# The first job of a transformer block on one core: 512 columns first, x from a second queue, and the operand split straight from PSUM

## The reference

```
xn   = rms_norm(x, norm_mix_g)
proj = xn @ w_in        # split: q_a k_a v_a | q_b k_b v_b | g_a g_b
o_a  = mixer_a(...)     # 16 heads of 64 on 2 key heads, window of 2 chunks, sink, t5 bias
o_b  = mixer_b(...)     # 16 heads of 64, chunks to the left, relative bias
merged = sigmoid(g_a) * (o_a @ w_branch_a) + sigmoid(g_b) * (o_b @ w_branch_b)
h    = x + merged @ w_out
hn   = rms_norm(h, norm_ffn_g)
out  = h + (silu(hn @ w_ffn_gate) * (hn @ w_ffn_up)) @ w_ffn_down
```

## Time and profile before

| | us |
|---|---|
| median of 3 runs (1349.22 to 1349.34) | 1349.26 |
| span of the profiled execution | 1347.3 |
| PE busy | 1331.1 (99%) |
| DVE busy | 743.3 (55%) |
| ACT busy | 606.4 (45%) |
| POOL busy | 33.5 (2%) |
| DMA: 251.23 MB, mean | 186 GB/s |

### The profile page before, as it was taken

The page is one execution under the profiler, slowest core; times in us unless marked ns, Lnnn a source line. Parts: engine busy times, 40 slices in busy tenths (PEclk is TensorE's granted clock), DMA queues, the critical chain, the costliest instruction groups (busy, mean ns, idle before and its releaser), DMA issues.

```text
span 1347.3 us, 16021 instructions
## 1 busy us (share of the span) xinstructions
PE 1331.1 (99%) x6224; PEld 1100.3 (82%) x6224; DVE 743.3 (55%) x938; ACT 606.4 (45%) x781; POOL 33.5 (2%) x34
## 2 busy tenths in 40 slices
PE   7999999999999999999999999999999999999998
PEld 6888887777788888888888888888888888888887
DVE  6556556777455555565555555455545554555553
ACT  5454545555444444444444443344444434444442
POOL 1112110000000000000000000000000000000000
PEclk9999999999999999999999999999999999999999
DMA  8655655444565555555565555555555556555552
GB/s 260 198 202 165 210 188 182 147 148 143 206 200 188 188 187 188 188 185 187 188 193 185 191 188 201 194 188 188 189 186 188 187 200 196 195 187 187 187 187 94
DMA packets 129943, 251.23 MB, mean 186 GB/s; under 512 B 4624, under 2 KB 10832, under 8 KB 129632
## 3 DMA queue, kind: packets, MB, share of 16 engines
q1 hardware_dynamic: 129600, 250.37, 56.5%
q0 software_dynamic: 288, 0.10, 0.1%
HBM read 248.33 MB, written 2.12 MB: 186 GB/s over the span
## 4 chain that ended last, share of the span: by engine, by line
PE 95%; ACT 3%; DVE 1%; issue 0%; DMA 0%; DVEq 0%; SPq 0%; ACTq 0%
PE bank L948 30%; PE bank L950 30%; PE bank L949 30%; PE bank L877 2%; ACT prob L594 1%; PE bank L892 1%; ACT w_hi L494 1%; PE bank L917 1%; DVE staged L657 0%; PE bank L919 0%; PE bank L902 0%; DMA x_rows<-in_x 0%; PE bank L918 0%; DVE xT_lo L665 0%; DVE w_lo L648 0%
## 5 line engine op out<-in xcount | busy, mean ns | idle before, releaser
L648 DVE TENSOR_TENSOR w_lo<-raw,w_hi 128x1024 fp32r<-128x1024 f32 (+1 forms) x464 | 562.5, 1216 | 556.1 <-ACT w_hi L494 554.2
L494 ACT ACTIVATE w_hi<-raw 128x1024 fp32r<-128x1024 f32 (+1 forms) x464 | 487.6, 1052 | 694.8 <-PE bank L950 693.2
L948 PE MATMUL bank<-w_hi,xT_hi 128*128 128x512 f32 (+1 forms) x1248 | 488.6, 391 | 4.2 <-DVE w_lo L648 3.0
L950 PE MATMUL bank<-w_lo,xT_hi 128*128 128x512 f32 (+1 forms) x1248 | 483.2, 387 | 0.0
L949 PE MATMUL bank<-w_hi,xT_lo 128*128 128x512 f32 (+1 forms) x1248 | 482.9, 387 | 0.0
L948 PEld LDWEIGHTS bank<-w_hi,xT_hi 128*128 128x128 f32 x1248 | 234.9, 188 | 53.7 <-issue 2.6
L950 PEld LDWEIGHTS bank<-w_lo,xT_hi 128*128 128x128 f32 x1248 | 234.9, 188 | 47.9
L949 PEld LDWEIGHTS bank<-w_hi,xT_lo 128*128 128x128 f32 x1248 | 235.1, 188 | 45.8
L948 PE MATMUL bank<-w_hi,oT_hi 128*128 128x512 f32 x480 | 187.0, 390 | 0.0
L950 PE MATMUL bank<-w_lo,oT_hi 128*128 128x512 f32 x480 | 186.8, 389 | 0.0
L949 PE MATMUL bank<-w_hi,oT_lo 128*128 128x512 f32 x480 | 186.7, 389 | 0.0
(11 more groups left out here) (109 smaller groups left out, 496.2 us busy)
## 6 DMA issues: line engine op xcount, KB each, us to landing
raw<-in_w_in SPq DMA_DIRECT2D x64, 1024.0 KB, 5.3
raw<-in_w_ffn_gate SPq DMA_DIRECT2D x44, 1024.0 KB, 5.2
raw<-in_w_ffn_up SPq DMA_DIRECT2D x44, 1024.0 KB, 5.1
raw<-in_w_ffn_down SPq DMA_DIRECT2D x44, 1024.0 KB, 5.0
raw<-in_w_out SPq DMA_DIRECT2D x16, 1024.0 KB, 5.0
raw<-in_w_branch_a SPq DMA_DIRECT2D x8, 1024.0 KB, 5.0
raw<-in_w_branch_b SPq DMA_DIRECT2D x8, 1024.0 KB, 4.9
x_rows<-in_x SPq DMA_DIRECT2D x4, 512.0 KB, 7.7
```

The lines of the kernel that those rows point to most:

```text
L494: A(w_hi[:, p % SPLIT_SLOTS, 0:w], raw[:, c % RAW_SLOTS, (p % 2) * w:(p % 2 + 1) * w], ACT.Copy).then_inc(hi_ready, 1)
L648: V.tensor_tensor(w_lo[:, p % SPLIT_SLOTS, 0:w], raw[:, p // 2 % RAW_SLOTS, (p % 2) * w:(p % 2 + 1) * w], w_hi[:, p % SPLIT_SLOTS, 0:w].bi ...
L948: M(sums, x_hi, w_hi[:, p % SPLIT_SLOTS, w], start=kt == 0, stop=False)
L950: ins = M(sums, x_hi, w_lo[:, p % SPLIT_SLOTS, w], start=False, stop=kt == j.kts - 1)
```

## The change

Four edits.

- `plan` puts the first 512-column qk job ahead of the kv job. The other jobs stay as they are.
- x and the norm weights (`mix_rows`) are loaded from ACT's queue, all at the start of ACT's program, instead of from SP's between the weight chunks.
- PE transposes x and h two k-tiles to a bank, all tokens of each, instead of four k-tiles of one half of the tokens. ACT reads the bank with the norm weight as scale into the `_hi` tile (`gained_to_hi`), and DVE multiplies the bank by the weight and subtracts the `_hi` tile in one instruction (`gained_to_lo`). `staged` is out of this path. In the first job this comes after the split of an even piece instead of ahead of it.
- The norm-weight transpose moves ahead of the first quarter of x, the third and fourth quarters are transposed after pieces 1 and 3 instead of 0 and 2, and the squares of x are summed in the second job's first two pieces.

The diff, cut to its core:

```diff
-    job("kv", 0, "w_in", 0, qa, 2 * kva, kt, "x", 0)
     for n in range(qa // COLS):
         job("qk", n, "w_in", 0, n * COLS, COLS, kt, "x", 0)
+        if n == 0:
+            job("kv", 0, "w_in", 0, qa, 2 * kva, kt, "x", 0)
...
             def do_job(j):
                 for q in range(j.pieces // 2):
-                    if j.prev is None:
-                        cs = slice(q * COLS, (q + 1) * COLS)
-                        sp.dma_start(x_rows[:, :, cs], x_view[:, :, cs]).then_inc(x_landed[q], 16)
                     load_chunk(j, q)
...
+            def gained_to_hi(first_bank, kt0, g0, pair0):
+                for i in range(GROUP // 2):
+                    act.wait_ge(x_turned, pair0 + i + 1)
+                    for c in range(2):
+                        kt = 2 * i + c
+                        ins = A(xT_hi[:, kt0 + kt, :], bank[first_bank + i][:, c * S:(c + 1) * S], ACT.Copy,
+                                scale=g_col[:, g0 + kt:g0 + kt + 1])
+                    ins.then_inc(gained_hi, 1)
...
-                if j.kind == "out" and k == 6:
-                    scaled_to_hi(NB + j.n, j.n)
+                if j.kind == "out" and k == 5:
+                    gained_to_hi(T_BANK, j.n * GROUP, KT + j.n * GROUP, KT // 2 + 2 * j.n)
...
+            act.dma_start(mix_rows[:], norm_mix_g[0].rearrange("(k p) -> k p", p=P)).then_inc(mix_landed, 16)
+            for q in range(NB):
+                cs = slice(q * COLS, (q + 1) * COLS)
+                act.dma_start(x_rows[:, :, cs], x_view[:, :, cs]).then_inc(x_landed[q], 16)
...
                 for k in range(j.pieces):
+                    split_hi(j, k)
                     if j.prev is None and k % 2 == 0:
-                        scaled_to_hi(k // 2, k // 2)
-                    split_hi(j, k)
-                    if j.prev is None and k in (5, 7):
+                        gained_to_hi(4 + 2 * (g % 2), g * GROUP, g * GROUP, 2 * g)
+                    if j.prev is jobs[0] and k < T:
...
+            def gained_to_lo(first_bank, kt0, g0, pair0):
+                for i in range(GROUP // 2):
+                    dve.wait_ge(gained_hi, pair0 + i + 1)
+                    for c in range(2):
+                        kt = 2 * i + c
+                        ins = V.scalar_tensor_tensor(xT_lo[:, kt0 + kt, :], bank[first_bank + i][:, c * S:(c + 1) * S],
+                                                     g_col[:, g0 + kt:g0 + kt + 1],
+                                                     xT_hi[:, kt0 + kt, :].bitcast(F32), ALU.mult, ALU.subtract)
+                    ins.then_inc(xT_ready, 1)
...
                 p = j.piece0 + k
                 hi, lo = lhs[j.lhs]
                 pe.wait_ge(lo_ready, p + 1 + j.off)
+                if j.prev is None:
+                    pe.wait_ge(xT_ready, k + 1)
...
-            turn_x(0)
             pe.wait_ge(mix_landed, 16)
             turn(bank[0][:, 0:KT], mix_rows[:], ident[0:KT, 0:KT]).then_inc(g_turned, 1)
+            turn_x(0)
             turn_x(1)
...
-                    if j.prev is None and k in (0, 2):
-                        turn_x(k // 2 + 2)
+                    if j.prev is None and k in (1, 3):
+                        turn_x((k - 1) // 2 + 2)
```

More of the change, by code:

```diff
@@ L135, in plan @@
             j.set = sets
-            sets += 1
+            sets += j.kind != "out"
     at = 0
@@ L611, in do_job @@
                 for k in range(j.pieces):
+                    split_hi(j, k)
                     if j.prev is None and k % 2 == 0:
[L613 to L615 removed]
+                        if k == 0:
+                            act.wait_ge(g_ready, 1)
+                        g = k // 2
+                        gained_to_hi(4 + 2 * (g % 2), g * GROUP, g * GROUP, 2 * g)
+                    if j.prev is jobs[0] and k < T:
                         for q in range(NB):
                             act.wait_ge(x_landed[q], 16)
[L618 to L620 removed]
+                        A(squares[:, k, :], x_rows[:, k, :], ACT.Square,
+                          accum_out=x_ss[:, k:k + 1]).then_inc(x_ss_ready, 1)
                     if j.prev is not None:
@@ L650, in split_lo @@
                                 w_hi[:, p % SPLIT_SLOTS, 0:w].bitcast(F32), ALU.subtract).then_inc(lo_ready, 1)
[L652 to L667, removed]
-                                ALU.subtract).then_inc(xT_ready, 1)
+            def gained_to_lo(first_bank, kt0, g0, pair0):
[7 more added lines that the diff above has]
+                    ins.then_inc(xT_ready, 1)
             def turned_to_lo(dst_hi, dst_lo, at_group, sets_before, ready):
@@ L733, in follow @@
                     if k == 5:
-                        dve.wait_ge(turned, j.set + 1)
-                        scale_rows(T_BANK, KT + j.n * GROUP, NB + j.n)
+                        gained_to_lo(T_BANK, j.n * GROUP, KT + j.n * GROUP, KT // 2 + 2 * j.n)
                         if j.n == NB - 1:
@@ L862, in turn_x @@
                 pe.wait_ge(x_landed[g], 16)
-                if g >= 2:
-                    pe.wait_ge(scaled_ready, g - 1)
-                for t in range(T):
-                    for c in range(GROUP):
-                        ins = turn(bank[4 + 2 * (g % 2) + t][:, c * P:(c + 1) * P],
-                                   x_rows[:, t, g * COLS + c * P:g * COLS + (c + 1) * P], ident[:])
-                ins.then_inc(x_turned, 1)
+                for i in range(GROUP // 2):
+                    if g >= 2:
+                        pe.wait_ge(xT_ready, 2 * (g - 2) + i + 1)
+                    for c in range(2):
+                        for t in range(T):
+                            col = g * COLS + (2 * i + c) * P
+                            ins = turn(bank[4 + 2 * (g % 2) + i][:, c * S + t * P:c * S + (t + 1) * P],
+                                       x_rows[:, t, col:col + P], ident[:])
+                    ins.then_inc(x_turned, 1)
             def turn_set(j):
                 pe.wait_ge(*staged_for(j))
-                src = h[:, :, columns(j)] if j.kind == "out" else staged
+                if j.kind == "out":
+                    for i in range(GROUP // 2):
+                        for c in range(2):
+                            for t in range(T):
+                                col = j.n * COLS + (2 * i + c) * P
+                                ins = turn(bank[T_BANK + i][:, c * S + t * P:c * S + (t + 1) * P],
+                                           h[:, t, col:col + P], ident[:])
+                        ins.then_inc(x_turned, 1)
+                    return
+                src = staged
                 for t in range(T):
```

21 lines of the change are left out of this document (7 added, 14 removed).

## The result

The changed kernel takes 1353.36 us (median of 7 runs, 1352.47 to 1353.90) against 1349.22 (7 runs, 1349.16 to 1349.34): 4.1 us slower, a ratio of 1.003 with an interval of 1.002 to 1.004. The forecast was 1350.3 with a range of 1347.6 to 1353.0. So the time lies just beyond the slow end. The runs also spread over 1.4 us, where those of the kernel before spread over 0.2: in the three shortest (up to 1353.18) the mean granted clock is 1.000, in the four others 0.998 or 0.999.

The account below looks back on a forecast made before the run. The prediction took PE's multiplies as the bound, with slack only in the opening. Later start +0.7, waits gone -2.4, slow pace 0 and new wait +2.8 made +1.1 on 1349.26: 1350.3 us, range 1347.6 to 1353.0.

Parts of the forecast that it names:

- The mark: Start of the third job's first multiply, forecast to move from 52.54 to 54.0 us.
- the owed transposes: Behind the mark: qk's head transposes are already done in place of kv's half set, giving back 0.4 us.
- The h part: The same staging replacement for h, where PE has no gap; costed at 0, a loss under 1.7 us.
- Even sharing of the queues from the start: Opening loads: both queues share evenly, so x's second quarter lands at 11.2 and the second weight chunk at 17.0 us.
- rival 3: Opening loads: weights served ahead of x, second quarter at 14.3, net +4.2, 1353.5 us; chance 0.12.
- later start: Opening: first multiply at 13.3 instead of 12.62 us, +0.7.
- The slow pace: First piece of multiplies runs at the 1.2 GHz pace, costing 1.1 us as before; change 0.
- rivals 1, 2 and 3: Opening loads: all landings 2.5 us earlier (1347.9), x served ahead (1349.9), weights served ahead (1353.5); chance 0.12 each.
- The waits for w_lo gone: Before the mark: PE's waits for DVE's w_lo and their tails vanish, -2.4 us.
- The new wait in the kv job: PE waits ahead of the head transposes because the norming chain outlasts kv's five pieces, +2.8 us.
- rival 5: kv job: head chain doesn't bind if POOL's steps run shorter, 1347.5 us; among others sharing chance 0.06.
- rival 4: kv job: the 2.8 us wait drops PE to the 1.2 GHz pace, costing 1.1, 1351.4 us; chance 0.06.

Follow-up runs that it names:

- b_queue: Kernel before with only the loads of x and the norm weights moved to ACT's queue at its start; 1350.52 us.
- a_kv_after_v: Changed kernel with the kv job moved from second place to behind the first v job; 1349.95 us.
- a_hold: Changed kernel with SP issuing the second weight chunk only once x's second quarter has landed; 1350.79 us.
- a_warm: Changed kernel with 14, 34 and 22 extra identity transposes where PE idles ahead of the first multiply; 1350.39 us.
- a_kvv_warm: Changed kernel with the kv job behind the first v job and extra identity transposes ahead of the first multiply; 1347.96 us.
- a_swap: Changed kernel with queues swapped: norm weights and x from SP's queue, the first four weight chunks from ACT's; 1352.00 us.
- a_mix_sp: Changed kernel with the 8 KB of norm weights moved to the head of SP's queue, x staying on ACT's; 1349.97 us.
- b_direct: Changed kernel with the new order and queue taken back, leaving the split from PSUM and the fourth edit; 1345.41 us.
- b_order: Kernel before with only the job order changed, first 512-column qk job ahead of kv; 1351.79 us.
- d_kvv: Changed kernel with x and the norm weights back in SP's queue and kv behind the first v job; 1349.00 us.
- a_x_on_sp: Changed kernel with x and the norm weights back in SP's queue between the weight chunks; 1351.65 us.

## Why the prediction was wrong, point by point

The sum was +1.1 us; the profiled spans differ by 3.4, the medians by 4.1. The profiled execution is one of the three shorter runs, which kept their clock; most of the other 0.7 is that the median isn't.

- **The mark and what lies behind it: right in the main.** From 52.54 to 56.06 is +3.5. Behind it the owed transposes should give 0.4 back, and 0.1 is left of that: one wait of PE for ACT's `probT` is new, 0.3 us at 269 us, in the attention. Every kernel in which ACT issues five transfers at its start shows it (b_queue, a_kv_after_v, a_hold, a_warm, a_kvv_warm and a_swap too), and none of the others does, a_mix_sp with four included. I have no cause for it. The h part is 0 (b_direct).
- **Even sharing of the queues from the start: the step that failed.** "I take them to share evenly, as nothing orders them", and from it x's second quarter at 11.2. Measured 13.0, and chunk 2 at 14.5 instead of 17.0. They share evenly from 6 us on, but until 4 us the weights ran nearly alone. The prediction named this case as rival 3, with 0.12, and put its decision point at 12.8 for the landing. The issue times gave a sign of the direction: SP's first weights at 0.73, x's first quarter at 1.2 behind the norm weights. They gave none of the size. The term "later start" was +0.7 and came to +2.0: the landing was 1.8 later than forecast, and the transposes ahead of the first multiply took 1.6 from start to start (13.03 to 14.65) where I had put 2.1, the length of their record.
- **That rival 3's time fits is partly luck.** Its landing was 14.3, not 13.0. With 13.0 its own rule, a us of PE for each us of x, gives 1350.3 + 1.8 = 1352.1, which is inside the range. The rest came from the next point and from the clock.
- **The slow pace: mis-sized.** I carried over 1.1 us and called the change in it 0. The first piece took 4.62 us from 14.65 to 19.27, where 2.72 is full pace: 1.9. How long it lasts isn't fixed: in the profiles of the kernels with a wide first job and no extra transposes 9 matmuls are slow in b_order, 8 in the changed kernel, 7 in a_swap, 4 in d_kvv, 3 in a_kv_after_v and a_mix_sp, 2 in a_x_on_sp and none in a_hold. The prediction had the 2.4 of a piece slow to its end and kept it "for the range", but the range is then made of rivals 1, 2 and 3 alone. A part of the spread over runs may be its doing; one trace for each kernel can't show that. a_warm takes it away together with the transposes' slow pace, and wins 2.4 us by that.
- **The waits for w_lo gone, -2.4: right to 0.3.** From 14.65 to 41.27 the parts make 26.4 (21.8, 1.8, 0.9, 1.9) and the trace has 26.6. But either edit takes them away: b_order has none with the old split and wide pieces, b_direct none with the new split and narrow ones. So beside the new order the new split brings nothing more; by itself (b_direct) it is worth 3.8 us, of which 2.0 is the earlier first multiply (10.60 instead of 12.62).
- **The new wait in the kv job: right in place, 2.4 from start to start for 2.8.** POOL's first step took 0.56 instead of 1.10 us, which is rival 5's condition for half a us of its 2.8, against "nothing makes them"; I have no cause for it. The earlier trace rows had 57.62 and 58.81, here it is:

```profile
45.93 0.56 POOL L459 TENSOR_SCALAR q_ms<-q_ss 128x16 f32<-128x16 f32 x1 [5.62 <-DVE q_ss L699]
46.58 2.93 POOL L460 TENSOR_TENSOR q_rs<-q_ms,minus_half 128x16 f32<-128x16 f32 x1
49.54 1.23 DVE L708 TENSOR_TENSOR staged<-side_a,q_rs 128x1024 f32<-128x1024 f32 x1 [3.11 <-POOL q_rs L460]
```

- **The fall of the clock behind that wait, rival 4 with 0.06: underrated.** It was absent in the changed kernel's profile and present in those of a_x_on_sp and a_warm. I priced it at 1.1; it was 1.5. It belongs to the spread between runs, and should have been part of the forecast's own range.
- **The instructions that replace `staged`: right.** Four on DVE took 1.67 us, for 1.7, and four on ACT 1.6. The split of rounding and subtracting is not where anything was lost.

```profile
11.37 1.67 DVE L666 SCALAR_TENSOR_TENSOR xT_lo<-bank,g_col,xT_hi 128x256 fp32r<-128x256 f32 x4 [3.51 <-ACT xT_hi L505]
```

Added up from these terms: +2.0 (start), +0.8 (slow pace), -2.1 (waits), +2.4 (new wait), +0.4 (full set of transposes for the half) make the 3.5 of the mark. Against the forecast that is 1.3 more for the start, 0.8 for the slow pace and 0.3 for the waits, and 0.4 less for the new wait.

Each part alone on the kernel before: order +2.5, queue +1.3, split -3.8, together 0.0 and not the +4.1 of all three. Put one on top of the other they do add up: order +2.5, then the split -0.1 (a_x_on_sp against b_order), then the queue +1.7 (the changed kernel against a_x_on_sp). The split's gain exists only with a narrow first job, where the chain through DVE and not the landing of x holds PE up.

## What to carry to other kernels

In an opening bound by loads, add up the bytes that stand ahead of the first operand that everything waits for, and begin with the job that needs the fewest. A second queue here moved the same bytes in another order, and the queue with the first large transfer ran nearly alone until 4 us, so give that place to what is needed first. Where an aftermath of fixed length (here the norming of the heads) is hidden under the next job, compare it with that job's time before a shorter job is put there.

## What the runs showed that I had not expected

- With two queues fed at the same time, one moved 0.45 to 0.49 MB between 1.5 and 4 us and the other 0.01 to 0.05, in both assignments; from 6 us on they were equal within 0.04 MB in 2 us. 8 KB moved from the head of one queue to the other's, which also made x's first transfer half a us earlier and the weights' half a us later, was worth 3.4 us.
- PE idle for 2.2 to 2.4 us in the middle of dense work was followed by the 1.2 GHz level in some profiles (a_x_on_sp, a_hold, a_warm) and not in others with a wait of the same length (the changed kernel, b_order, a_mix_sp, and a_hold itself in its kv job). In the first microseconds the pace is that of the low level although the clock column reads 1.00.
- 26 transposes that compute nothing, in time that was idle, gave 1.7 us in one kernel, and 70 gave 3.0 in another, 2.4 of them before any difference in the clock later on.
